# Three value projections in four tiles of 512 columns instead of eight of 256

## The reference, cut to what matters

```python
# first block
h = rms_norm(x, mix_norm_g)
proj = h @ w_in                      # fq, fk, fv, flog, dq, dk, dv side by side
fox_out  = fox_attention(fq, fk, fv, log_sigmoid(flog + b_forget))   # 8 heads of 64
diff_out = diff_attention(dq, dk, dv, lam, slopes)                   # 4 heads, values 128 wide
x = x + concat(fox_out, rms_norm(diff_out)) @ w_out
x = x + (silu(h2 @ w_gate) * (h2 @ w_up)) @ w_down
# second block
z = rms_norm(x, norm1_g) @ w_in_2 + b_in_2     # q, k, v, c_a, c_b, g_a, g_b
br_a = neighbourhood_attention(q, k, v, rpb) @ w_na_out              # 8 heads of 64
u = depthwise_conv_31_taps(c_a * sigmoid(c_b)); br_b = silu(layer_norm(u)) @ w_conv_out
x = x + (sigmoid(g_a) * br_a + sigmoid(g_b) * br_b) @ w_out
x = x + (gelu(conv3(gate)) * conv3(val)) @ w_down
```

## Time and profile before

| | before |
|---|---|
| median of the runs | 1490.25 us |
| profiled execution, first to last instruction (span) | 1484.2 us |
| median less span | 6.05 us |
| PE / PEld busy | 1410.8 us (95%) / 1137.6 us (77%) |
| DVE / ACT / POOL busy | 832.1 us / 600.8 us / 552.8 us |
| PE share of the chain that ended last | 23%, DVE 15%, issue 6%, ACT 3% |
| matmuls | 6620 |

### The profile page before, as it was taken

One profiled execution on the slowest core, in us unless ns is written; L12 is line 12 of the kernel. 1 busy time (PEld: TensorE's weight loads), 2 busy tenths in 40 slices (PEclk: granted clock), 3 DMA queues, 4 the chain that ended last, 5 costly groups with the idle time before them and its releaser, 6 DMA issues. The chain is left out here.

```text
span 1484.2 us, 18829 instructions
## 1 busy us (share of the span) xinstructions
PE 1410.8 (95%) x6620; PEld 1137.6 (77%) x6620; DVE 832.1 (56%) x1229; ACT 600.8 (40%) x928; POOL 552.8 (37%) x242
## 2 busy tenths in 40 slices
PE   7999999989999999999799999979999999999998
PEld 5877887667888888888588778757777777778887
DVE  6677656565222222223388777987547777775011
ACT  5344443365444342333433544434344433333223
POOL 4421132133444444445153113434434444444441
PEclk9999999999999999999899999989999999999999
DMA  5221121012333332333632112212222223332331
GB/s 146 77 56 37 44 71 58 29 57 76 110 97 99 99 99 88 97 92 98 102 99 72 58 43 72 85 58 84 86 85 85 85 85 93 92 97 80 101 97 63
DMA packets 223630, 120.70 MB, mean 81 GB/s; under 512 B 15172, under 2 KB 222417, under 8 KB 223569
## 3 DMA queue, kind: packets, MB, share of 16 engines
q1 hardware_dynamic: 223569, 119.89, 28.4%
HBM read 117.56 MB, written 2.31 MB: 81 GB/s over the span
## 5 line engine op out<-in xcount | busy, mean ns | idle before, releaser
L515 POOL TENSOR_TENSOR WL<-RAW,WH 128x1024 fp32r<-128x1024 f32 (+1 forms) x220 | 547.0, 2493 | 899.8 <-ACT WH L1049 899.6
L640 PE MATMUL PS<-XH,WH 128*128 128x512 f32 x1088 | 439.8, 404 | 33.1 <-DVE T L2008 14.4
L642 PE MATMUL PS<-XH,WL 128*128 128x512 f32 x1088 | 426.8, 392 | 0.0
L641 PE MATMUL PS<-XL,WH 128*128 128x512 f32 x1088 | 426.3, 392 | 0.0
L1049 ACT ACTIVATE WH<-RAW 128x1024 fp32r<-128x1024 f32 (+1 forms) x220 | 227.9, 1037 | 321.0 <-PE PS L642 281.8
L640 PEld LDWEIGHTS PS<-XH,WH 128*128 128x128 f32 x1088 | 206.7, 190 | 85.5 <-DVE T L2008 22.4
L642 PEld LDWEIGHTS PS<-XH,WL 128*128 128x128 f32 x1088 | 205.5, 189 | 44.1
L641 PEld LDWEIGHTS PS<-XL,WH 128*128 128x128 f32 x1088 | 206.0, 189 | 39.7 <-issue 0.7
L640 PE MATMUL PS<-HH,WH 128*128 128x512 f32 (+1 forms) x374 | 141.1, 377 | 0.0
L642 PE MATMUL PS<-HH,WL 128*128 128x512 f32 (+1 forms) x374 | 141.0, 377 | 0.0
L641 PE MATMUL PS<-HL,WH 128*128 128x512 f32 (+1 forms) x374 | 141.0, 377 | 0.0
(11 more groups left out here) (305 smaller groups left out, 1996.4 us busy)
## 6 DMA issues: line engine op xcount, KB each, us to landing
RAW<-in_w_up SPq DMA_DIRECT2D x66, 512.0 KB, 3.8
RAW<-in_w_in SPq DMA_DIRECT2D x60, 512.0 KB, 3.9
RAW<-in_w_down SPq DMA_DIRECT2D x32, 512.0 KB, 4.0
RAW<-in_w_gate SPq DMA_DIRECT2D x22, 512.0 KB, 3.8
RAW<-in_w_out SPq DMA_DIRECT2D x16, 512.0 KB, 3.6
RAW<-in_w_down SPq DMA_DIRECT2D x16, 384.0 KB, 3.5
XTM<-in_x SPq DMA_DIRECT2D x4, 512.0 KB, 6.4
RAW<-in_w_na_out SPq DMA_DIRECT2D x4, 512.0 KB, 3.4
```

What stands on the lines that cost most here:

```text
L515: pool.tensor_tensor(WL[:, s, 0:width], RAW[:, s % 2, 0:width], WH[:, s, 0:width].bitcast(F32), ALU.subtract).then_inc(w_lo, 1)
L640: pe.matmul(out, ah, bh, start=start, stop=False)
L641: pe.matmul(out, ah, bl, start=False, stop=False)
L642: return pe.matmul(out, al, bh, start=False, stop=stop)
```

## The change

V1, V2 and V3 have four tiles each instead of eight, one for each block of 128 tokens and all 512 columns of values. Their units are two chunks by 512 columns, so every tile reads all four units, and a unit is free when the last tile has passed its two chunks. ACT's `hi_next` for the first two units stands behind the copy of tile 2, for the other two behind the copy of tile 3. V2 has a tile in step 32 and one in step 34 of the first attention, and two behind it. What was called behind one of eight tiles is called behind one of four: `log_forget` and `gate_logs` at new places, and four taps instead of two behind a V3 tile. Constants that count tiles (`TL`, `PT0`, `per`) and the waits built on them follow; `v_take`'s wait for an earlier low part goes, since four tiles fill the four buffers `T`.

```diff
@@ -63,7 +63,7 @@
     u = []
-    v = lambda m, c0: [(m, 4 * k, 4, c0 + 256 * h, 256) for h in range(2) for k in range(2)]
+    v = lambda m, c0: [(m, 2 * k, 2, c0, 512) for k in range(4)]
     col = lambda m, c0: [(m, 0, 8, c0, 128)]
     FOX_Q, FOX_K, FOX_V, DQ, DK, DV = 0, 512, 1024, 1544, 2056, 2568
     u += col("w_in", FOX_Q) + col("w_in", FOX_K)
...
@@ -571,8 +571,8 @@
         if kind == "fox":
             for f in range(8):
                 add("qk", f, a + f, u + f, *qk_steps[f])
-            for i in range(3):
-                add("v", i, TL["v2"] + i, UN["v2"], N_SCORES + i, N_SCORES + i, False, PT0["v2"] + i + 1)
+            for i in range(2):
+                add("v", i, TL["v2"] + i, UN["v2"], N_SCORES + 2 * i, N_SCORES + 2 * i, False, PT0["v2"] + i + 1)
         elif kind == "na":
             for f in range(6):
                 add("qk", f, a + f, u + f, *qk_steps[f])
...
@@ -678,18 +678,18 @@
         def v_tile(name, i):
-            half, t, a = i // TC, i % TC, TL[name] + i
-            pe.wait_ge(w_lo, UN[name] + 2 * half + 2)
+            a, q = TL[name] + i, slice(i * P, (i + 1) * P)
             need_acc(a)
             for k in range(KD):
-                u = UN[name] + 2 * half + k // 4
-                w = slice((k % 4) * 256, (k % 4) * 256 + 256)
-                ins = mm3(PS[:, ACC + a % 2, 0:256], XH[:, k, t * P:(t + 1) * P], XL[:, k, t * P:(t + 1) * P],
-                          WH[:, u % 4, w], WL[:, u % 4, w], k == 0, k == KD - 1)
-
-            if t == TC - 1:
-                ins.then_inc(w_used, 2)
-            else:
+                u = UN[name] + k // 2
+                if k % 2 == 0:
+                    pe.wait_ge(w_lo, u + 1)
+                w = slice((k % 2) * S, (k % 2) * S + S)
+                ins = mm3(PS[:, ACC + a % 2, :], XH[:, k, q], XL[:, k, q], WH[:, u % 4, w], WL[:, u % 4, w],
+                          k == 0, k == KD - 1)
+                if k % 2 and i == TC - 1:
+                    ins.then_inc(w_used, 1)
+            if i < TC - 1:
                 ins.then_inc(part_ready, 1)
         def norm_sum(ss, which=0):
...
@@ -748,7 +748,7 @@
         for t in range(TC):
             ins = pe.transpose(PS[:, TRB + 1, 8 * t:8 * t + 8], FLR[0:8, t * P:(t + 1) * P], IDF[0:8, 0:8])
         ins.then_inc(fl_ps, 1)
-        for i in range(1, 6):
+        for i in range(1, 3):
             v_tile("v1", i)
...
@@ -758,8 +758,7 @@
                 ins = pe.matmul(PS[:, TRB + 1, :], part[:, t, :], TRI[:, 384 - P * t:896 - P * t],
                                 start=(t == 0 and i == 0), stop=(t == TC - 1 and i == 1))
         ins.then_inc(cum_ps, 1)
-        for i in range(6, 8):
-            v_tile("v1", i)
+        v_tile("v1", 3)
         def attention(kind):
             f = FAM[kind]
...
@@ -1084,16 +1083,17 @@
             if n_pv:
                 act.wait_ge(pv_ready, n_pv)
-            for i in range(8):
+            for i in range(4):
                 a = TL[name] + i
                 act.wait_ge(acc_free, a + 1)
                 if hook:
                     hook(i)
-                c0 = 256 * (i // 4)
-                act.activation(mem["VH"][:, i % 4, c0:c0 + 256], tile_t(a, 256), ACT.Copy).then_inc(act_done, 1)
-                if i % 4 == 3:
-                    hi_next(UN[name] + 2 * (i // 4))
-                    hi_next(UN[name] + 2 * (i // 4) + 1)
+                act.activation(mem["VH"][:, i, :], tile_t(a), ACT.Copy).then_inc(act_done, 1)
+                if i == 2:
+                    hi_next(UN[name])
+                    hi_next(UN[name] + 1)
+            hi_next(UN[name] + 2)
+            hi_next(UN[name] + 3)
         def qk_part(kind, a, par, i, bias=None):
             buf = FAM[kind]["mem"]["QH" if i % 2 == 0 else "KH"]
...
@@ -1115,7 +1115,7 @@
             qk_part("fox", TL["fox0"] + i, 0, i)
         def gate_logs(i):
-            if i == 3:
+            if i == 1:
                 act.wait_ge(fl_step, 2)
                 act.activation(LAM[:, 2:4], LAM[:, 0:2], ACT.Exp).then_inc(fl_act, 1)
                 act.wait_ge(fl_step, 8)
...
@@ -1123,7 +1123,7 @@
                 act.wait_ge(fl_act, 2)
                 act.activation(Z[:, 2, :], Z[:, 2, :], ACT.Ln, bias=1.0).then_inc(fl_act, 1)
-            if i == 6:
+            if i == 3:
                 act.wait_ge(cum_ps, 1)
                 act.wait_ge(cr_dve, 1)
...
@@ -1488,27 +1487,25 @@
         def v_take(name, i, bias=False):
-            a, c0, t = TL[name] + i, 256 * (i // 4), i % 4
+            a = TL[name] + i
             tile_ready(name, i)
-            if i >= 4:
-                dve.wait_ge(low_done, L0[name] + i - 3)
             if bias:
-                dve.scalar_tensor_tensor(out=tile_t(a, 256), in0=ps(a, 256), scalar=RT[:, t:t + 1],
-                                         in1=BVB[:, c0:c0 + 256], op0=ALU.mult, op1=ALU.add).then_inc(acc_free, 1)
+                dve.scalar_tensor_tensor(out=tile_t(a), in0=ps(a), scalar=RT[:, i:i + 1],
+                                         in1=BVB[:, :], op0=ALU.mult, op1=ALU.add).then_inc(acc_free, 1)
             else:
-                dve.tensor_scalar(tile_t(a, 256), ps(a, 256), RT[:, t:t + 1], None, ALU.mult).then_inc(acc_free, 1)
+                dve.tensor_scalar(tile_t(a), ps(a), RT[:, i:i + 1], None, ALU.mult).then_inc(acc_free, 1)
         def v_phase(name, mem, bias, extra=None, taken=0):
             if taken == 0:
                 slots_drained(name)
-            for i in range(8 + 1):
-                if taken <= i < 8:
+            for i in range(4 + 1):
+                if taken <= i < 4:
                     v_take(name, i, bias)
                 if i >= 1:
-                    a, c0, t = TL[name] + i - 1, 256 * ((i - 1) // 4), (i - 1) % 4
+                    a, t = TL[name] + i - 1, i - 1
                     dve.wait_ge(act_done, H0[name] + i)
-                    dve.tensor_tensor(mem["VL"][:, t, c0:c0 + 256], tile_t(a, 256), mem["VH"][:, t, c0:c0 + 256].bitcast(F32),
+                    dve.tensor_tensor(mem["VL"][:, t, :], tile_t(a), mem["VH"][:, t, :].bitcast(F32),
                                       ALU.subtract).then_inc(low_done, 1)
                 if extra:
                     extra(i)
...
@@ -1539,7 +1536,7 @@
         def log_forget(i):
-            if i == 1:
+            if i == 0:
                 dve.wait_ge(fl_ps, 2)
                 for t in range(TC):
                     dve.tensor_tensor(Z[:, 0, 8 * t:8 * t + 8], PS[:, TRB + 1, 8 * t:8 * t + 8], BFG[:, :],
...
@@ -1548,16 +1545,16 @@
                 dve.scalar_tensor_tensor(out=Z[:, 1, :], in0=Z[:, 0, :], scalar=-1.0, in1=Z[:, 0, :], op0=ALU.mult,
                                          op1=ALU.max).then_inc(fl_step, 1)
                 dve.tensor_scalar(Z[:, 3, :], Z[:, 0, :], 0.0, None, ALU.min).then_inc(fl_step, 1)
-            if i == 4:
+            if i == 2:
                 dve.wait_ge(fl_act, 3)
                 dve.tensor_tensor(Z[:, 2, :], Z[:, 2, :], Z[:, 3, :], ALU.subtract).then_inc(fl_step, 1)
                 dve.wait_ge(fl_step, 9)
                 nlf = Z[:, 2, :].rearrange("p (t h) -> p t h", h=8)
-                for i, c in enumerate((0, 32)):
+                for n, c in enumerate((0, 32)):
                     dve.tensor_copy(LFH[:, :, c:c + 8], nlf).then_inc(fl_step, 1)
-                    dve.wait_ge(fl_step, 10 + i)
+                    dve.wait_ge(fl_step, 10 + n)
                     dve.tensor_tensor(LFL[:, :, c:c + 8], nlf, LFH[:, :, c:c + 8].bitcast(F32), ALU.subtract).then_inc(lf_ready, 1)
-            if i == 5:
+            if i == 2:
                 dve.wait_ge(fl_act, 1)
                 dve.tensor_tensor(LAM[:, 4:5], LAM[:, 3:4], LAM[:, 2:3], ALU.subtract).then_inc(lam_ready, 1)
...
@@ -1565,12 +1562,12 @@
                 dve.tensor_scalar(LAM[:, 5:6], LAM[:, 4:5], LAM_INIT, None, ALU.subtract).then_inc(lam_ready, 1)
                 dve.tensor_copy(RI[:, 0:1], BT[:, :]).then_inc(cr_dve, 1)
-            if i == 7:
+            if i == 3:
                 dve.wait_ge(cr_act, 2)
                 dve.tensor_tensor(CR[32:40, :], PS[32:40, TRB + 1, :], CT[32:40, :].bitcast(F32),
                                   ALU.subtract).then_inc(cr_dve, 1)
-            if i == 2:
+            if i == 1:
                 dve.wait_ge(rpb_in, 16 * RPR)
                 dve.tensor_scalar(RPP[:, :], RPP[:, :], -1.0, None, ALU.mult).then_inc(rpb_negated, 1)
...
@@ -1778,8 +1775,8 @@
             clause(2, diff_, ALU.is_le, 23.0), combine(1, 2, ALU.mult), as_mask(2)]
         attention("fox", R[:, :], lambda i: mask_steps[i]() if i < len(mask_steps) else None)
-        v_take("v2", 3)
-        v_phase("v2", M1, False, taken=4)
+        v_take("v2", 2)
+        v_phase("v2", M1, False, taken=3)
         attention("diff", R[:, :])
         diff_normed(3)
         diff_low(3)
...
@@ -1913,7 +1910,7 @@
             conv_taps(4)
         rt_copy(2)
         dve.wait_ge(bv_in, 16)
```

(11 more changed lines are left out.)

12 lines of the change are left out of this document (6 added, 6 removed).

## The result

The changed kernel takes 1498.54 us (median of 6 runs, 1496.39 to 1501.63) beside 1488.93 (6 runs, 1485.09 to 1490.84): 1.0074 of before, 95% interval 1.004 to 1.0109. Measured again: 1498.18 (12 runs) beside 1487.22, 1.0084 (1.0053 to 1.0114). The recorded ratios are not the quotients of these medians, which are 1.0065 and 1.0074; between the medians lie 9.6 and 11.0 us, by the ratios it would be 11.0 and 12.5. It is slower, by some 10 to 12 us, under 1%; forecast was +10.7.

The account below looks back on a forecast made before the run. TensorE bounds 830 to 925 us, then DVE to 988, so a delay entering the third attention passes in full. +1.6 + 0.8 + 5.6 + 2.7 = +10.7 makes the span 1494.9, with 6.05 around it about 1501 us; range 1489 to 1506.

Parts of the forecast that it names:

- Widths: All three value projections: 512-column matmuls save 1.25 us per projection, 3.75 us for the three.
- V1, +1.6: First projection: late gate split and gate step delay the scores, +1.6 us; bounds -1.25 and +3.5 (clock fall).
- V2, +0.8: Second projection: scores begin 1.25 us earlier, but late unit loads delay ACT's first exponential; scores 2 +0.8 us.
- V3, +5.6 and +2.7: Third projection: DVE instructions blocked by POOL's conversions delay scores 2 by 5.6 us; half clock after 8 us idle adds 2.7.
- half the jam: Rival, V3: tile 3 later against conversions, or clock holds; one or two blocked taps and 2.7 go; +5.8, 1496; chance 0.15.
- DVE keeps the port: Rival, V3: queued taps go ahead of POOL, attention begins 0.4 us earlier than before; 1492.3 us; chance 0.06.
- TensorE decides: Rival, all three projections: columns save 3.75 us, conversions stay hidden; faster, 1486.3 us; chance 0.12.
- Nothing: Rival, whole kernel: gains of 3.75 us and a smaller delay cancel; 1490 us; chance 0.07.
- The absolute time: Whole run: forecast span of 1494.9 us plus the 6.05 us around it, about 1501 us.

Follow-up runs that it names:

- only_v3: Against the kernel before, only the third value projection has four tiles of 512 columns: 1.0038 of before (1.0021 to 1.0055).
- late_taps: Changed kernel with V3's 16 taps as 6, 6, 4, 0 and ACT's late conversions behind exponentials of the attention: 0.999 of before (0.9967 to 1.0013).
- um_v3: Changed kernel with V3's four tiles opened with the first two units, then closed one by one, and 10 taps ahead of the first take: 1.0018 of before.
- V2 alone: Against the kernel before, only the second value projection has four tiles of 512 columns: 0.9968 of before, measured again 0.9967.

## Why the prediction was right

- **Widths.** V2's tiles alone: scores 0 begin 24.70 us behind the start instead of 25.89, -1.2 (expected -1.25).
- **V1, +1.6: right, measured +2.05.** Idle ahead of the gate matmuls 2.31 (2.5), scores 0 at 70.97 (70.7 to 70.9), first exponential from 75.98 (done at 76). That nothing more is lost behind it fits, since scores 0 alone account for +1.9 to +2.05 of it. The clock fell in this profile, which cost 1.35 more and was in the bounds, not in the forecast. In the times of whole runs with V1 alone wide the +2 us do not show (median +0.1).
- **V2, +0.8: right, +0.9.** First exponential 31.71 us behind V2's start, which is 205.1 for the start forecast (204.9).
- **V3, +5.6 and +2.7 = +8.3: right, +5.8 to +9.1.** Tile 0 waited 3.80 (3.6). The end of V3 came 0.7 earlier instead of 2.4: half clock lasted 6.8 us behind the wait, not 3.4; in only_v3, where it lasted 3.4, the end came 2.4 earlier. The four blocked instructions, the first maximum (40.38 behind the start; forecast 39.15) and the idle time (7.54; forecast 8) came as worked out. Scores 2 came +6.8 us (forecast +5.6); half clock then lasted 6.4 us of work (5.5), and scores 3 stood 5.92 us behind scores 2 instead of 3.25, which is the +2.7. In the second profile of the changed kernel POOL's last two conversions ran later, from 814.46, and only two instructions were blocked ahead of the first maximum (36.42 behind the start, +3.5, close to the 3 us below which the prediction called itself wrong). ACT's exponential, behind its own two conversions, was then the last to be ready, and scores 2 came +4.2 us. That is the rival *half the jam*, within V3 alone. It is a draw of one and the same kernel, so the two together, and not either profile, bear out the +8.3.
- **DVE keeps the port** did not happen: POOL began at 804.43, and the tap that came up at 805.05 stood 2.90 us; the two conversions took 5.76 us, where a pair in V2 takes 4.74. The Trainium skill ("SBUF — State Buffer", Who interferes with whom) calls the port pair that DVE and GpSimd share "an exclusive lock". The trace agrees as far as it goes: each engine's instruction was lengthened by the other's, and in each of the four cases one DVE instruction passed per conversion.
- **TensorE decides** fell by the result, and only_v3 and late_taps show where: the widths win only where nobody waits for units. **Nothing** fell by the interval.
- **The absolute time** was less well founded than the difference. The 6.05 us "around" the span are not around it: a run's time is 1.8 us over its own span in every run of the changed kernel (1.8 to 2.9 in those of before). The other 4 us say that the profiled execution of before was shorter than the median one. Measured again, before was 1487 to 1489 us and not 1490.25. The two errors went opposite ways: +10.7 on the medians then measured would be 1498 to 1500.

What the forecast did not have is the variation of the loading stage and the clock's fall in V1, together 4.5 us of the single profile's +13.4, and the -2.84 of the rest, most of which is a long last stage in the profile of before. In the sum itself V1 was put 0.45 us too low, the V3 of single profiles lay 2.5 below and 0.8 above its term, and the 1.0 us that comes back behind V3 was not in it. That these come out near zero, and +10.7 so close to the +9.6 and +11.0 of the medians, is in part luck; the mechanisms are not.

## What to carry to other kernels

When a tile grows, ask how long its operands are held: a buffer given back only by the last tile moves all following loads and conversions to the end of the stage, in front of the next stage's first steps. Two remedies are worth a try: other work queued ahead of the jam and the conversions behind the first exponentials (late_taps), or all tiles opened with the first units and then closed, which gives the units back early (um_v3). The second needs every bank free at the start, and here a wait of 3 us moved from inside the projection to its front. So mark a stage by the end of the engine's last wait before it, not by its first instruction. And before a microsecond of one profile is booked on a change, look for the same step in a kernel that does not have it.

## What the runs showed of the hardware

- A fall of TensorE's clock (2.4 to 1.2 GHz) came or stayed away at the same place of the same code: between V1 and V2, 0, 3.4 or 6.8 us of it with the old V1 in four profiles. They took 132.5 and 132.7, 134.07 and 135.66 us, so 3.4 us at half clock cost about 1.5 us.
- Sixteen small loads on SP's queue took 18.9 to 22.9 us from the first issue to the last in 14 profiles of the same 16 instructions (`BNR`), and the unit load that stands behind them was issued that much later. That sets TensorE's idle time of 6.5 to 12.4 us; what sets the pace of the issues is open.
- Beside a POOL subtraction of 128 x 1024 (2.39 to 2.42 us alone), a DVE instruction that reads two tensors of 128 x 512 in SBUF took 1.8 to 2.9 us instead of 0.7, one such instruction for each subtraction. DVE's take out of PSUM between them stayed at 0.74 us.
- The last feed-forward ran gapless in one of 14 profiles and 14 us faster. The short runs (6 of 111 of before below 1480 us, 6 of 24 of V2 alone) may be this; that was not shown run by run.
